# Hybrid RWKV-7 / latent-attention / mixture-of-experts block: two expert loads held behind the first gather, one head pair loaded in series, a transpose moved behind the down products

## The reference

```
h = modulate(rmsnorm(x)); z = h @ w_in                  # split into three parts
y_rwkv = rwkv7_branch(...)                              # 8 heads of 64, a scan over the tokens
y_mla  = mla_branch(...)                                # 8 heads, q and k of 96, v of 64, causal softmax
merged = sig(g1) * (y_rwkv @ wb1) + sig(g2) * (y_mla @ wb2)
x = x + gt_m * (merged @ w_out)
h2 = modulate(rmsnorm(x))
g_idx = argmax(h2 @ w_rg + b_rg)                        # 1 of 4 groups
top_w, top_i = top_k(softmax(e_logits[g_idx]), 2)       # 2 of the 8 experts of the group
for e in range(32):                                     # D_EXPERT = 256
    hid = silu(h2 @ w_e_gate[e]) * (h2 @ w_e_up[e])
    out = out + combine[:, e] * (hid @ w_e_down[e])
x = x + gt_f * out
```

## Time and profile before

| | us |
|---|---|
| median of 3 runs | 1557.85 |
| lowest, highest | 1556.87, 1561.06 |
| the profiled execution's own time | 1559.73 |
| its span, first to last instruction | 1557.9 |

### The profile page before, as it was taken

The page is one execution under the profiler, slowest core; times in us unless marked ns, Lnnn a source line. Parts: engine busy times, 40 slices in busy tenths (PEclk is TensorE's granted clock), DMA queues, the critical chain, the costliest instruction groups (busy, mean ns, idle before and its releaser), DMA issues. The chain is left out here.

```text
span 1557.9 us, 32809 instructions
## 1 busy us (share of the span) xinstructions
PE 1389.4 (89%) x14293; PEld 993.7 (64%) x14293; DVE 771.8 (50%) x1122; ACT 496.2 (32%) x908; POOL 258.7 (17%) x301
## 2 busy tenths in 40 slices
PE   3799999976999998799989999999994799999990
PEld 0497777744899998577777888787884233333330
DVE  0654767656667665455557555656455112111215
ACT  1542322353334344443445444323111111111110
POOL 0001212203656552011110000000000111111110
PEclk7899999986999999899999999999996799999995
DMA  9841223261000001660003113414108699999958
GB/s 361 298 141 48 81 62 88 61 235 45 4 4 4 4 11 36 171 229 15 15 15 149 54 54 115 184 67 153 41 38 348 230 362 417 414 418 411 407 216 325
DMA packets 80828, 246.56 MB, mean 158 GB/s; under 512 B 8872, under 2 KB 42152, under 8 KB 63920
## 3 DMA queue, kind: packets, MB, share of 16 engines
q1 hardware_dynamic: 73344, 227.70, 39.4%
q0 software_dynamic: 7344, 16.79, 2.8%
HBM read 216.13 MB, written 38.29 MB: 163 GB/s over the span
## 5 line engine op out<-in xcount | busy, mean ns | idle before, releaser
L2913 PE MATMUL ps<-gu,xT 128*32 128x512 f32 x1536 | 176.9, 602 | 1.3 <-ACT xT L2994 0.7
L3102 DVE TENSOR_TENSOR sg<-sg,ps 128x256 f32<-128x256 f32 x25 | 10.5, 421 | 213.0 <-ACT sg L2999 213.0
L2913 PEld LDWEIGHTS ps<-gu,xT 128*32 128x32 f32 x1536 | 47.9, 111 | 106.8 <-issue 102.8
L351 PE MATMUL ps<-hh,wr_h 128*128 128x512 f32 x224 | 93.2, 416 | 0.5 <-DVE wr_l L347 0.5
L352 PE MATMUL ps<-hl,wr_h 128*128 128x512 f32 x224 | 88.5, 395 | 0.0
L353 PE MATMUL ps<-hh,wr_l 128*128 128x512 f32 x224 | 88.5, 395 | 0.0
L2931 PE MATMUL ps<-dn,hidT 128*32 128x512 f32 x768 | 86.8, 592 | 0.5 <-ACT hidT L3003 0.5
L2021 DVE TENSOR_REDUCE nmax<-ps 128x1 f32<-128x896 f32 (+4 forms) x64 | 45.8, 752 | 72.5 <-PE ps L1919 71.9
L1404 DVE TENSOR_TENSOR inverses<-inverses,ps 128x512 f32<-128x512 f32 (+1 forms) x80 | 49.9, 630 | 54.4 <-PE ps L1627 54.0
L1189 POOL TENSOR_TENSOR off<-mats,cst 128x256 f32<-128x256 f32 x80 | 66.4, 847 | 50.7 <-PE ps L1611 50.6
L1627 PE MATMUL ps<-inverses,xx 64*64 64x64 f32 x1280 | 71.3, 218 | 0.0
(11 more groups left out here) (419 smaller groups left out, 3339.1 us busy)
## 6 DMA issues: line engine op xcount, KB each, us to landing
gu<-w_e_gate SPq DMA_DIRECT2D x34, 1024.0 KB
gu<-w_e_up SPq DMA_DIRECT2D x34, 1024.0 KB
dn<-w_e_down SPq DMA_DIRECT2D x34, 1024.0 KB, 13.4
wbuf<-w_ada SPq DMA_DIRECT2D x16, 1024.0 KB, 11.1
wbuf<-w_ada SPq DMA_DIRECT2D x16, 512.0 KB, 5.3
wraws<-w_gates SPq DMA_DIRECT2D x16, 512.0 KB, 4.8
rows<-expert_rows SPq DMA_DIRECT2D x16, 512.0 KB, 9.4
wr<-w_rwkv SPq DMA_DIRECT2D x14, 512.0 KB, 3.6
```

Source lines behind the costliest of these rows:

```text
L351: nc.tensor.matmul(out, wt[0], mov[0], start=(k == 0), stop=False)
L2913: last = nc.tensor.matmul(ps[part, GB[b]], xT[:, b, k, part], gu[:, expert(m, c_) % WB, :, k], start=(k == 0), stop=(k == KD - 1))
```

## The change

Three edits. The numbers of lines behind them shift by 4 to 7 in the changed kernel.

1. SP holds the six transfers of experts 3 and 4 until the first gather has landed. The request for the row `gt` stands behind them in SP's list as before.
2. The three transfers of head pair 0 are issued one after the other, each when the one before has landed. The other pairs keep their way.
3. In a turn of the overflow loop TensorE transposes `hid` and computes the down products before it transposes the next rows, and ScalarE copies in the same order.

```
+HELD = 3
...
-        def load_pair(sp, p):
+        def load_pair(sp, p, one_by_one=False):
...
             sp.dma_start(qT[0:QKD, two], rows_q).then_inc(pair_in[p], 16)
+            if one_by_one:
+                sp.wait_ge(pair_in[p], 16)
             sp.dma_start(kT[0:QKD, two], rows_k).then_inc(pair_in[p], 16)
+            if one_by_one:
+                sp.wait_ge(pair_in[p], 32)
             sp.dma_start(vv[:, :, two], ...).then_inc(pair_in[p], 16)
...
-                    load_pair(sp, 0)
+                    load_pair(sp, 0, True)
...
                 for e in range(1, WB):
+                    if e == HELD:
+                        sp.wait_ge(xg_in[0], 16)
                     load_gate_up(e)
                     load_down(e)
                 sp.wait_ge(tb_s, 1)
...
                 with pe.Fori(0, n) as i:
                     gate_up(i)
+                    hidden_transposes(i + FIXED, 0)
+                    down(i)
                     row_transposes(i + (FIXED + 1), 0, 2 * i + (2 * FIXED + 2), ..., over_gu)
-                    hidden_transposes(i + FIXED, 0)
-                    down(i)
...
                     gates(m, 0)
+                    hidden_out(m, 0)
                     rows_in(m + 1, 0)
-                    hidden_out(m, 0)
```

## The result

The changed kernel is slower: 1560.7 us (1557.44 to 1565.2, 20 runs) beside 1557.05 us for the one before on the same chips, ratio 1.0025 with a 95% interval of 1.0017 to 1.0034. The forecast was 1557.0, which from its base of 1557.85 is 0.8 us faster, no change that can be told. Measured is 3.6 us slower. The value lies in the range, but the sign was missed: I had the gain of edit 2 and the loss of edit 1 nearly cancel, and the loss is larger.

The account below looks back on a forecast made before the run. The prediction took TensorE, busy for 89% of the span, as the bound and aimed at its idle stops. Edits 2, 1 and 3 summed as -3.1 + 2.3 + 0 = -0.8 us, from 1557.85 to 1557.0; range 1551.5 to 1562.3.

Parts of the forecast that it names:

- 2.1 us of the stop: TensorE's instruction pause at 622.25 us: series loading of pair 0 was to save 2.1 of its 3.76 us.
- the net was 3.1: Edit 2 at head pair 0: 4.6 us saved less 1.5 for a second pause, 3.1 us faster, between 0 and 6.3.
- The second pause of 1.5 us: After TensorE resumes near 622 us, its next instruction piece was to queue behind the keys, costing 1.5 us (0 to 3).
- the 2.5 us of clock: Behind the pause at 622 us: a shorter pause was to leave TensorE's clock up, saving 2.5 us.
- The 1.3 us between piece and restart: At the 622 us pause: TensorE was taken to go on some 1.3 us after its instruction piece came in.
- the start that I took, 621.3: Pair 0 in series: the instruction piece was to start about 621.3, where the queries' last data pass.
- The 6.3 us that I said hang on the stop: At 622.25 us: the 3.76 us pause plus 2.5 us lost to low clock behind it, together 6.3 us.
- The gather's gain: Start of the expert phase: with experts 3 and 4 held, the first gather was to land 4.5 us earlier.
- The price of the clock: Lower TensorE clock behind the pause for `gt` in the expert phase: 2.2 us lost, between 1.2 and 3.5.
- the time from the gather to `gt`: Expert phase, SP's queue: 7.9 MB at 408 to 422 GB/s, 18.8 us plus 2.0 fixed, `gt` landing at 1232.8.
- The 1.8 us that I named as its upper bound: Overflow pass: the clock could fall for the down products after 1.5 us idle, priced 0 to 1.8 us, taken as 0.
- Rival (c): Expert phase: pause for `gt` 6 us with low clock, 5.0 us lost, edit 2 giving 0: 1562.9 us; chance 0.13.

Follow-up runs that it names:

- e1: Edit 2 alone (head pair 0 in three pieces in series) on the kernel before: 1553.44 us, ratio 0.998.
- e4: The changed kernel with the row `gt` requested ahead of the held transfers of experts 3 and 4: 1550.12 us, ratio 0.9965 against the kernel before.
- e8: The kernel before with pair 0 requested in one go, only after TensorE's last state inputs: 1551.14 us, ratio 0.9956.
- e11: e9 with the overflow pass in the new order: 1546.35 us, ratio 0.992 against the kernel before.
- e2: Edit 1 alone (experts 3 and 4 held until the first gather has landed) on the kernel before: 1561.73 us, ratio 1.0035.
- e3: Edit 3 alone (overflow pass transposes the next rows behind the down products) on the kernel before: 1555.82 us, ratio 1.0002.
- e5: Edit 1 alone with only expert 4 held, three transfers ahead of `gt`, on the kernel before: 1553.76 us, ratio 0.9975.
- e6: The kernel before with pair 0 in series and experts 3 and 4 held behind `gt`, overflow pass in old order: 1550.17 us, ratio 0.9954.
- e7: The kernel before with pair 0 in series and only expert 4 held, ahead of `gt`, overflow pass in old order: 1548.87 us, ratio 0.9952.
- e9: The kernel before with pair 0 requested later in one go, experts 3 and 4 held behind `gt`, overflow pass in old order: 1546.89 us, ratio 0.9934.
- e10: e9 with only expert 4 held behind `gt`: 1545.89 us, ratio 0.992 against the kernel before.

## Why the prediction was wrong, point by point

**Edit 2** was right in mechanism and nearly in size: 2.1 us of the stop were to go, 1.9 went; the net was 3.1, measured 2.4 in the profile and 2.7 in the runs of e1. Two of its terms were wrong and offset each other. The second pause of 1.5 us did not come (e4 has one of 0.35 us, the others none), and the 2.5 us of clock were not saved in every profile. e8 shows that the cause is the pair's traffic in front of the instructions, and the table above that the 16 KB piece is late by about as much as TensorE stops. The 1.3 us between piece and restart were read from the end of a window; by the narrow windows it is 2.7 us. This changed nothing in the sum, because the start that I took, 621.3, was right: the changed kernel's piece is counted at 621.4 to 621.5. The 6.3 us that I said hang on the stop are confirmed too: e8 to e11 reach the first scores 6.0 to 6.2 us sooner, counted from the same row.

**Edit 1** had the right new wait in the right place: `gt` behind six transfers, VectorE held, TensorE's pause, low clock behind it. The gather's gain was put at 4.5 us and measured 4.4. The price of the clock was 2.2, measured 2.5. The step that failed is the time from the gather to `gt`: 7.9 MB at 408 to 422 GB/s, 18.8 us, with 2.0 us around it. From the first transposes of the gathered rows to `gt` it was to be 20.8 us and was 23.7 (1209.72 to 1233.4). In that time 9.2 MB moved, not 7.9. The gathers had 1.40 MB instead of 1.07, and SP's queue had 7.82 instead of 6.82, since part of expert 5's gate and up weights, requested at 1222.48, moved before the last of `gt`. And the rate was 262 and 341 GB/s in the windows up to 1218, and 388 over the whole stretch; 408 to 422 had been read in a stretch whose queues were already full. By my estimate from these numbers the 1.3 MB more are 3.1 us at the forecast's rate and the lower rate is 1.8 us, and nothing is left for the fixed 2.0. The pause was 8.55 us where 4.6 were forecast: 2.9 us by the later `gt`, and 1.1 because TensorE's work between gather and pause took 16.1 us and not 17.2 (the clock rose earlier), which only lengthened the pause. So edit 1 cost 5.6 us in both measurements instead of 2.3. The forecast for edit 1 alone reached to 5 us slower, and e2 lies just outside.

**Edit 3** was right in that nothing starts sooner: TensorE stands 1.49 us where the transposes lay. The 1.8 us that I named as its upper bound came up in three of the four profiles with the new order (1.7 us) and in none of the nine with the old one. But e3 and e11 show no cost in the median (1.0002, and 1546.35 beside 1546.89), so how often the clock falls there stays open.

**The sum** was -3.1 + 2.3 + 0. By the medians of the single edits it was -2.7, +5.6 and -0.3: +2.6, beside +3.6 measured for all. The difference of 1 us is inside the intervals, which are 2.5 to 3 us either way for each single edit. The cause of the miss is the one term of edit 1. Rival (c) had the mechanism and nearly the size of that loss (5.0 us) and got 0.13. Its point of decision, `gt` landing later than 1234.5, was written for a phase that isn't shifted; with the 2.4 us of edit 2 taken out, `gt` landed at 1235.8.

## What to carry to other kernels

When a bulk request is held back to let an urgent transfer through, list what is queued behind the held request on the same issuing engine: the next small transfer that somebody waits for has to be issued ahead of it (here some 9 us between the two orders). A transfer put into the middle of a dense stretch of TensorE can stop it through its instructions; here a later request cured that better than the same pieces in series. A pause is priced with the clock behind it. How long a transfer takes in a queue is priced with everything that moves in the meantime, later requests too, and with a rate read where queues fill up, not where they are full.

## What the runs showed of the hardware

TensorE's stop for instructions went with the transfers under way when its next piece was due: 3.76 to 4.31 us with all three transfers of the pair requested (before, e2, e3, e5), 1.56 to 1.84 with only the first (changed, e1, e4, e6, e7), none with no transfer (e8 to e11).

The long stops were followed by a granted clock of 0.50 over the next 5.1 us in all four profiles. The short ones were followed by 1.00 in e1, e4 and e6, and by a mean of 0.67 in the changed kernel and e7: the same code at this place, two outcomes. In the overflow pass it was the same with 1.48 to 1.49 us of idle time in front of the transposes of `hid`: 0.53 to 0.65 in three profiles, 1.00 in one.

A transfer of 512 KB landed 19.4 to 19.8 us after its request behind six transfers of 1 MB (changed, e2), 14.1 to 14.6 us behind three (e5, e7), and 6.5 to 7.1 us ahead of them (e4, e6, e9, e10, e11).
